# Attention scores: rotary high halves as paired 64-row products, and one maximum over four banks

## The chip, the cores and the metric

The kernel runs on one core of a Trainium2 chip. The metric is device time in microseconds (us) of one launch; the kernel before takes 2313.79 us, the median of 3 runs (2311.18 to 2315.13). The engines run their own instruction lists and meet through semaphores: TensorE (PE, matrix products; PEld is its weight load), VectorE (DVE), ScalarE (ACT), GpSimd (POOL) and SyncE (SP, which issues the transfers).

## The reference

Two layers of an encoder on 2048 tokens of width 1024, all in float32. The first is a retention branch beside an attention branch, the second a convolution module. The change lies in the attention: 4 heads, each query and key the concatenation of 128 plain and 64 rotary numbers, the rotary key shared by all heads, softmax over all 2048 keys.

```python
q = jnp.concatenate([q[..., :128], _rope(q[..., 128:], cos, sin)], axis=-1)
k = jnp.concatenate([k_nope, jnp.broadcast_to(k_rope, (B, S, MLA_HEADS, MLA_ROPE_DIM))], axis=-1)
s = jnp.einsum('bqhd,bkhd->bhqk', qblk, k, preferred_element_type=jnp.float32) * scale
p = jax.nn.softmax(s, axis=-1).astype(v.dtype)
o = jnp.einsum('bhqk,bkhd->bqhd', p, v)
```

## The kernel before

Products are made from float32 numbers that are each split into a rounded high part (type fp32r) and a low rest. A product of two split operands is the sum of low*high, high*low and high*high.

The function `attention` runs 16 groups n (4 heads of 4 groups of 512 queries), each in 4 blocks b of 128 queries. In a block, TensorE makes the scores of 128 queries against 2048 keys in four pieces of 512 keys (`scores`, kb 0 to 3), one PSUM bank each, of five products: plain low*high, high*low, two rotary ones, plain high*high. The rotary operand `q_rot` has the 64 high rows on partitions 0 to 63 and the 64 low rows on partitions 64 to 127. `kr_swap` holds the key's rotary parts as low over high and `kr_same` as high over low, so that a product of 128 rows with `kr_swap` gives high*low + low*high, and one with `kr_same` gives high*high + low*low.

Between the scores of block b, TensorE works on the group before: `turn` transposes the softmax weights (`probs`) of four key tiles kt, `values_of` multiplies them with the values. All orders are written out by hand. Per block: scores 0, turn 0, scores 1, turn 1, scores 2, scores 3, values -2, values -1, turn 2, values 0, turn 3, values 1; negative numbers are tiles that the block before has turned. Group 0 has no group before it, and in its odd blocks the scores go to the four other banks.

VectorE takes a maximum of each bank as it is finished (`block_max`), then one of the four results, and scales it to `bias` (`block_bias`); ScalarE takes the four exponentials (`exps`) in the block after, the first of them behind `turn_hi` of turn 2. `turn_hi` (ScalarE) and `turn_lo` (VectorE) split what TensorE has turned. Scores of piece kb wait until the exponential of the block before has read that bank (`exp_done`); turn kt waits for `turn_lo` of kt - 2 (`ptlo_done`).

In block 1 VectorE also splits the queries of the next group (`split_q`) and, in the group after a head's first, a quarter of the values (`split_v`), before `turn_lo` of tile 3. In block 3 it adds a piece of the second layer's modulation weights, loaded by SP in block 0, to the sum `acc`. The first queries are split earlier, in `q_high` and `q_low`.

Of the kernel before, what the change touches and what calls it, by code (L numbers as in the profile page):

```python
# [12 lines left out]
F32 = mybir.dt.float32  # L13
# [1381 lines left out]
def q_high(dve, begun, early, q_in):  # L1395
    q_st, qr_st = early[0:2]
    dve.wait_ge(q_in, 48)
    dve.tensor_copy(begun.q_rot[:], qr_st[:]).then_inc(begun.rot_hi, 1)
    dve.tensor_copy(begun.q_hi[:], q_st[:]).then_inc(begun.qhi_done, 1)


def q_low(dve, begun, early):
    q_st, qr_st = early[0:2]
    dve.wait_ge(begun.rot_hi, 1)
    dve.tensor_tensor(begun.q_rot[ROPE:P, :], qr_st[ROPE:P, :], begun.q_rot[ROPE:P, :].bitcast(F32),
                      ALU.subtract).then_inc(begun.rot_ready, 1)
    dve.wait_ge(begun.qhi_done, 1)
    dve.tensor_tensor(begun.q_lo[:], q_st[:], begun.q_hi[:].bitcast(F32), ALU.subtract).then_inc(begun.qlo_first, 1)


def first_scores(nc, ctx, base, early_at):

    KB = 1024
    f = Store()

    def at(name, offset, n):
        return nc.alloc_sbuf_tensor_at(name, [P, n], F32R, offset=offset)

# [12 lines left out]
    return f  # L1431


def attention(nc, st, ada_w, acc, kr_keep, early_at, early, k_in, q_in, begun, w_out, w_raw, w_lo, mix, mix_in, xt, x, x_in, out_stored):
# [4 lines left out]
    with ExitStack() as ctx:  # L1439
# [24 lines left out]
        q_hi, q_lo, q_rot = [[one] for one in (begun.q_hi, begun.q_lo, begun.q_rot)]  # L1464
        for name, pair in (("hi", q_hi), ("lo", q_lo), ("rot", q_rot)):
            sb(f"q_{name}_place", [P, GQ])
            pair.append(sb(f"q_{name}1", [P, GQ], F32R))
        probs = [[sb(f"probs{i}{b}", [P, S]) for b in range(QB)] for i in range(2)]
# [5 lines left out]
        ada = sb("ada2", [P, 3 * D // 2])  # L1474
        mx = sb("mx", [P, QB])
# [21 lines left out]
        max_done = sem("max_done")  # L1497
# [25 lines left out]
        ada_view = ada_w.rearrange("(k p) (a n) -> k a p n", p=P, a=2)  # L1523
# [39 lines left out]
        def bank_of(n, b, kb):  # L1563

            return (ps_pt + ps_o)[kb][:] if first(n) and b % 2 else ps_s[kb][:]
# [18 lines left out]
        def _(sp):  # L1584
# [12 lines left out]
            def group(n, s, score, values, write):  # L1597
# [4 lines left out]
                for b in range(QB):  # L1602
# [44 lines left out]
        def _(act):  # L1647
# [14 lines left out]
            def turn_hi(m, kt):  # L1662
                act.wait_ge(pt_done, 16 * m + kt + 1)
                if not (isinstance(m, int) and 16 * m + kt < 4):
                    act.wait_ge(pv_done, 16 * m + kt - 3)
                act.activation(pt_hi[kt % 4][:], ps_pt[kt % 2][:], ACT.Copy).then_inc(pthi_done, 1)  # L1666
# [11 lines left out]
            def group(n, s, score, values, write):  # L1678
                for b in range(QB):
# [13 lines left out]
                    if b == 1 and write:  # L1693
                        act.wait_ge(pv_done, 16 * (n - 1))
                        if not isinstance(n, int) or n > 2:
                            act.wait_ge(o_turned, n - 2)
                        act.activation(o_t[:], ps_o[s][:], ACT.Copy).then_inc(o_out, 1)
# [44 lines left out]
        def _(dve):  # L1742
# [6 lines left out]
            def split_q(m, sl):  # L1749
# [6 lines left out]
                dve.tensor_tensor(q_rot[sl][ROPE:P, :], qr_st[ROPE:P, :], q_rot[sl][ROPE:P, :].bitcast(F32),  # L1756
                                  ALU.subtract).then_inc(rot_ready, 1)
# [11 lines left out]
            def turn_lo(m, kt):  # L1769
                hold(dve, st, pthi_done, 16 * m + kt + 1)  # L1770
                dve.tensor_tensor(pt_lo[kt % 4][:], ps_pt[kt % 2][:], pt_hi[kt % 4][:].bitcast(F32),  # L1771
                                  ALU.subtract).then_inc(ptlo_done, 1)

            def group(n, s, score, values, write):
                for b in range(QB):
# [3 lines left out]
                    if b == 3 and score:  # L1779
                        hold(dve, st, ada_in, 16 * (n + 1))  # L1780
                        half = slice(s * 3 * D // 2, (s + 1) * 3 * D // 2)
                        if isinstance(n, int) and n < 2:
                            dve.tensor_scalar(acc[:, half], ada[:], st.silu_c[:, 0:1], None, ALU.mult).then_inc(acc_done, 1)
                        else:
                            hold(dve, st, acc_done, n - 1)
                            dve.scalar_tensor_tensor(acc[:, half], ada[:], st.silu_c[:, bass.ds(n // 2, 1)],
                                                     acc[:, half], ALU.mult, ALU.add).then_inc(acc_done, 1)
                    for i in range(4):
                        if score:
                            block_max(n, b, i)  # L1790
                        if i < 2 and turned:
                            turn_lo(turned[0], turned[1] + i)
# [30 lines left out]
        def _(pe):  # L1823
            def scores(n, s, b, kb):
# [24 lines left out]
                pe.matmul(dst, q_rot[s][:, q], kr_same[:, k], start=False, stop=False)  # L1849
                pe.matmul(dst, q_hi[s][:, q], k_hi[hs][:, k], start=False, stop=True).then_inc(s_done, 1)  # L1850
# [10 lines left out]
            def values_of(m, sl, kt):  # L1861
# [5 lines left out]
                pe.matmul(ps_o[sl][:], v_lo[:, kt, :], pt_hi[kt % 4][:], start=kt == 0, stop=False)  # L1867
                pe.matmul(ps_o[sl][:], v_hi[:, kt, :], pt_lo[kt % 4][:], start=False, stop=False)  # L1868
                pe.matmul(ps_o[sl][:], v_hi[:, kt, :], pt_hi[kt % 4][:], start=False, stop=kt == NK - 1).then_inc(pv_done, 1)  # L1869

            def group(n, s, score, values, write):
                for b in range(QB):
# [13 lines left out]
                    if score:  # L1886
# [5 lines left out]
                        scores(n, s, b, 3)  # L1892
                        values_next(-2)
# [1201 lines left out]
```

## Time and profile before

| | |
|---|---|
| median of 3 runs | 2313.79 us |
| the profiled execution's own time | 2312.47 us |
| its span (first to last instruction) | 2310.6 us |
| granted TensorE clock, mean share of full speed | 0.989 |
| TensorE busy, share of the span | 97% |
| VectorE, ScalarE, GpSimd busy | 59%, 49%, 39% |

The profile is of one execution. A busy matrix product is not TensorE at its peak: products are pipelined, so the distance between the starts of two of them, not the length of one, is what each costs. In a timeline row the bracket says how long the engine stood idle just before, and which instruction ended that.

### The profile page before, as it was taken

What the parts mean: (1) busy time and instruction counts of PE and PEld (TensorE: products, weight loads), DVE (VectorE), ACT (ScalarE), POOL (GpSimd) and SP (SyncE); (2) the same over time, 40 slices, a digit from 0 to 9 for tenths busy, and PEclk for the clock granted to TensorE, in tenths of its full rate; (3) what the DMA queues carried; (4) which work ended last, traced back from release to release, by engine and by line L of the source; (5) the groups of instructions that cost most, each with busy time, mean ns of one, the idle gap of its engine ahead of it and who ended that gap; (6) DMA issues with size and microseconds to landing.
All of it is one profiled execution on the core that took longest, in us unless ns stands there. A gap on an engine that the chain in (4) does not pass through costs nothing. (4 is left out here: it accounts for less than half of the span.)

```text
span 2310.6 us, 31013 instructions
## 1 busy us (share of the span) xinstructions
PE 2242.0 (97%) x11298; PEld 1884.8 (82%) x11298; DVE 1370.0 (59%) x2083; ACT 1125.9 (49%) x2095; POOL 900.6 (39%) x665
## 2 busy tenths in 40 slices
PE   5999999999999999999999989998999999999998
PEld 5888888898897788888888878887888888888886
DVE  7333336343435776767677642115999999994442
ACT  5555534222224555555555535556555566663432
POOL 6322222232222111101101023232999999992454
PEclk9999999999999999999999999999999999999999
DMA  7533323534444222222131323331111211145553
GB/s 304 183 136 136 136 78 132 173 120 151 137 149 141 56 65 69 65 69 65 32 83 33 105 105 112 134 118 37 46 55 42 69 55 42 64 167 163 157 172 101
DMA packets 151298, 245.75 MB, mean 106 GB/s; under 512 B 8964, under 2 KB 95236, under 8 KB 146566
## 3 DMA queue, kind: packets, MB, share of 16 engines
q1 hardware_dynamic: 146566, 235.73, 31.0%
q10 hardware_dynamic: 4608, 8.39, 1.0%
q8 instruction: 75, 1.23, 0.2%
q14 instruction: 49, 0.40, 0.1%
HBM read 157.84 MB, written 86.25 MB: 106 GB/s over the span
## 5 line engine op out<-in xcount | busy, mean ns | idle before, releaser
L2410 POOL TENSOR_TENSOR conv_g<-conv_g,product 128x1024 f32<-128x1024 f32 x160 | 385.0, 2408 | 34.2 <-ACT product L2459 24.5
L2554 DVE SCALAR_TENSOR_TENSOR ps_b<-u,cols,ps_b 128x1024 f32<-128x1024 f32 x304 | 391.7, 1288 | 9.2
L2670 PE MATMUL ps_a<-ho_hi,wp_lo 128*128 128x512 f32 x768 | 300.2, 391 | 6.8 <-DVE h_left L2610 6.8
L2671 PE MATMUL ps_a<-h_left,wp_hi 128*128 128x512 f32 x768 | 299.6, 390 | 0.0
L2672 PE MATMUL ps_a<-ho_hi,wp_hi 128*128 128x512 f32 x768 | 299.5, 390 | 0.0
L2459 ACT ACTIVATE product<-u,cols 128x1024 f32<-128x1024 f32 x160 | 183.3, 1151 | 170.3 <-POOL conv_g L2410 169.0
L1771 DVE TENSOR_TENSOR pt_lo<-ps_pt,pt_hi 128x512 fp32r<-128x512 f32 x256 | 176.1, 688 | 136.0 <-ACT pt_hi L1666 134.0
L1666 ACT ACTIVATE pt_hi<-ps_pt 128x512 fp32r<-128x512 f32 x256 | 154.4, 604 | 202.9 <-PE ps_pt L1858 202.1
L1761 DVE TENSOR_REDUCE mx<-ps_s 128x1 f32<-128x512 f32 x248 | 168.2, 683 | 34.3 <-PE ps_s L1850 32.6
L1659 ACT ACTIVATE probs<-ps_s,bias 128x512 f32<-128x512 f32 x248 | 168.8, 700 | 17.6 <-DVE bias L1767 9.3
L2670 PEld LDWEIGHTS ps_a<-ho_hi,wp_lo 128*128 128x128 f32 x768 | 144.6, 188 | 38.6 <-DVE h_left L2610 8.7
L2672 PEld LDWEIGHTS ps_a<-ho_hi,wp_hi 128*128 128x128 f32 x768 | 144.6, 188 | 30.1
L2671 PEld LDWEIGHTS ps_a<-h_left,wp_hi 128*128 128x128 f32 x768 | 144.4, 188 | 29.8
L1721 POOL TENSOR_TENSOR q_lo<-q_st,q_hi 128x512 fp32r<-128x512 f32 x15 | 26.9, 1793 | 342.6 <-DVE q_hi L1754 342.6
L1858 PEld LDWEIGHTS ps_pt<-const,probs 128*128 128x128 f32 x1024 | 127.0, 140 | 38.1 <-DVE pt_lo L1771 4.7
L1858 PE MATMUL ps_pt<-const,probs 128*128 128x128 f32 x1024 | 154.0, 273 | 2.1 <-DVE pt_lo L1771 2.1
L1846 PE MATMUL ps_s<-k_hi,q_lo 128*128 128x512 f32 x248 | 111.0, 448 | 7.6 <-ACT probs L1659 5.0
L1867 PE MATMUL ps_ot<-pt_hi,v_lo 128*128 128x512 f32 x256 | 111.9, 437 | 0.3 <-DVE pt_lo L1771 0.3
L2924 PE MATMUL ps_a<-w_last_hi,mo_lo 128*128 128x512 f32 x256 | 101.1, 395 | 1.8 <-PEq L2200 1.7
L1869 PE MATMUL ps_ot<-pt_hi,v_hi 128*128 128x512 f32 x256 | 100.7, 393 | 0.0
L1868 PE MATMUL ps_ot<-pt_lo,v_hi 128*128 128x512 f32 x256 | 100.2, 391 | 0.0
L2926 PE MATMUL ps_a<-w_last_hi,mo_hi 128*128 128x512 f32 x256 | 99.9, 390 | 0.0
(445 smaller groups left out, 5435.4 us busy)
## 6 DMA issues: line engine op xcount, KB each, us to landing
scratch_ret_pack<-pack SPq DMA_DIRECT2D x14, 1280.0 KB, 5.5
pack<-scratch_ret_pack SPq DMA_DIRECT2D x14, 1280.0 KB, 6.4
ada<-in_ada_w_dram SPq DMA_DIRECT2D x16, 768.0 KB, 6.1
wp_raw<-in_od_w_in_dram SPq DMA_DIRECT2D x24, 512.0 KB, 3.9
xt<-in_x_dram SPq DMA_DIRECT2D x16, 512.0 KB, 6.2
ada<-in_ada_w_dram SPq DMA_DIRECT2D x8, 1024.0 KB, 9.3
mix_e<-scratch_mix SPq DMA_DIRECT2D x16, 512.0 KB, 4.5
x_e<-in_x_dram SPq DMA_DIRECT2D x16, 512.0 KB, 5.0
```

The source lines that it names most:

```text
L1659: act.activation(probs[s][b][:, kb * BANK:(kb + 1) * BANK], bank_of(n, b, kb), ACT.Exp, bias=bias[b % 2][:], scale=SCALE, accum_out=sums[s ...
L1666: act.activation(pt_hi[kt % 4][:], ps_pt[kt % 2][:], ACT.Copy).then_inc(pthi_done, 1)
L1761: dve.tensor_reduce(mx[:, kb:kb + 1], bank_of(n, b, kb), AX.X, ALU.max).then_inc(max_done, 1)
L1771: dve.tensor_tensor(pt_lo[kt % 4][:], ps_pt[kt % 2][:], pt_hi[kt % 4][:].bitcast(F32), ALU.subtract).then_inc(ptlo_done, 1)
L1858: mm = pe.transpose(ps_pt[kt % 2][:, qb * P:(qb + 1) * P], probs[sl][qb][:, kt * P:(kt + 1) * P], ident)
L1867: pe.matmul(ps_o[sl][:], v_lo[:, kt, :], pt_hi[kt % 4][:], start=kt == 0, stop=False)
L2410: pool.tensor_tensor(half(conv_g, h), half(conv_g, h), product[adds(c, i, h) % 2][:], ALU.add).then_inc(added, 1)
L2459: act.activation(product[adds(c, i, h) % 2][:], units(c, V_TAPS + i, h), ACT.Copy, scale=tap_w).then_inc(product_done, 1)
L2554: dve.scalar_tensor_tensor(acc[h], units(c, k, h), params(c, k), acc[h], ALU.mult, ALU.add).then_inc(tap, 1)
L2670: pe.matmul(dst, lo[:, k, :], h_hi[:, k, t], start=k == 0, stop=False)
L2671: pe.matmul(dst, hi[:, k, :], h_lo[:, k, t], start=False, stop=False)
L2672: mm = pe.matmul(dst, hi[:, k, :], h_hi[:, k, t], start=False, stop=k == KD - 1)
```

## The change

The product with `kr_same` goes out of the five. In its place come, behind the four products of all four banks, four products of 64 rows (`high_scores`): banks 0 and 2 with the high rows of `q_rot` and `kr_same` on partitions 0 to 63, banks 1 and 3 with a new copy `q_high` of the high query rows and the high key rows of `kr_swap` on partitions 64 to 127. low*low is no longer computed. Only these four signal that a bank is ready. VectorE takes one maximum over the four banks in one instruction of 2048 columns, behind `turn_lo` 0 and 1. The cast of the rotary queries becomes two casts of 64 rows. The modulation weights come in pieces of 768 columns, in blocks 0 and 2, and are added in blocks 1 and 3.

```diff
+    f.q_high = at("q_high0", f.kr_at + 26 * KB, BANK)
-        ps_s = [bank(f"ps_s{i}") for i in range(4)]
-        ps_pt = [bank(f"ps_pt{i}") for i in range(2)]
-        ps_o = [bank(f"ps_ot{i}") for i in range(2)]
+        ps_all = [ctx.enter_context(nc.psum_tensor(n, [P, QB * BANK], F32)) for n in ("ps_scores", "ps_turned")]
+        banks = [[four[:, i * BANK:(i + 1) * BANK] for i in range(QB)] for four in ps_all]
+        ps_s, ps_pt, ps_o = banks[0], banks[1][0:2], banks[1][2:4]
...
-                    if b == 0 and score:
-                        hold(sp, st, acc_done, n)
-                        sp.dma_start(ada[:], ada_view[n // 2][s]).then_inc(ada_in, 16)
+                    if b % 2 == 0 and score:
+                        sp.wait_ge(acc_done, 2 * n + b // 2)
+                        sp.dma_start(ada[:], ada_view[n // 2][2 * s + b // 2]).then_inc(ada_in, 16)
...
-                dve.tensor_copy(q_rot[sl][:], qr_st[:]).then_inc(rot_hi, 1)
+                dve.tensor_copy(q_rot[sl][0:ROPE, :], qr_st[0:ROPE, :])
+                dve.tensor_copy(q_high[sl][ROPE:P, :], qr_st[ROPE:P, :]).then_inc(rot_hi, 1)
...
-            def block_max(n, b, kb):
-                hold(dve, st, s_done, 16 * n + 4 * b + kb + 1)
-                dve.tensor_reduce(mx[:, kb:kb + 1], bank_of(n, b, kb), AX.X, ALU.max).then_inc(max_done, 1)
-
             def block_bias(n, b):
-                hold(dve, st, max_done, 16 * n + 4 * b + 4)
-                dve.tensor_reduce(m1[:], mx[:], AX.X, ALU.max).then_inc(m1_done, 1)
+                dve.wait_ge(s_done, 16 * n + 4 * b + 4)
+                dve.wait_ge(bias_ready, 4 * n + b)
+                four = ps_all[1 if first(n) and b % 2 else 0]
+                dve.tensor_reduce(m1[:], four[:], AX.X, ALU.max).then_inc(m1_done, 1)
...
-                pe.matmul(dst, q_rot[s][:, q], kr_same[:, k], start=False, stop=False)
-                pe.matmul(dst, q_hi[s][:, q], k_hi[hs][:, k], start=False, stop=True).then_inc(s_done, 1)
+                pe.matmul(dst, q_hi[s][:, q], k_hi[hs][:, k], start=False, stop=False)
+
+            def high_scores(n, s, b):
+                q = slice(b * P, (b + 1) * P)
+                for kb in range(QB):
+                    k = slice(kb * BANK, (kb + 1) * BANK)
+                    if kb % 2 == 0:
+                        mm = pe.matmul(bank_of(n, b, kb), q_rot[s][0:ROPE, q], kr_same[0:ROPE, k], start=False, stop=True)
+                    else:
+                        mm = pe.matmul(bank_of(n, b, kb), q_high[s][ROPE:P, q], kr_swap[ROPE:P, k], start=False, stop=True)
+                    mm.then_inc(s_done, 1)
...
                         scores(n, s, b, 3)
+                        high_scores(n, s, b)
                         values_next(-2)
```

TensorE, scores 3 of a block and what follows them, before (`ps_s` is a score bank, `ps_ot` the output):

```order
L1846 MATMUL ps_s<-k_hi_1684,q_lo 128x512
L1847 MATMUL ps_s<-k_lo_1685,q_hi 128x512
L1848 MATMUL ps_s<-kr_swap,q_rot 128x512
L1849 MATMUL ps_s<-kr_same,q_rot 128x512
L1850 MATMUL ps_s<-k_hi_1684,q_hi 128x512
L1867 MATMUL ps_ot<-pt_hi,v_lo 128x512
```

The same place now (`ps_scores` are the four score banks, `ps_turned` the four others):

```order
L1850 MATMUL ps_scores<-k_hi_1684,q_lo 128x512
L1851 MATMUL ps_scores<-k_lo_1685,q_hi 128x512
L1852 MATMUL ps_scores<-kr_swap,q_rot 128x512
L1853 MATMUL ps_scores<-k_hi_1684,q_hi 128x512
L1860 MATMUL ps_scores<-kr_same,q_rot 128x512
L1862 MATMUL ps_scores<-kr_swap,q_high 128x512
L1860 MATMUL ps_scores<-kr_same,q_rot 128x512
L1862 MATMUL ps_scores<-kr_swap,q_high 128x512
L1880 MATMUL ps_turned<-pt_hi,v_lo 128x512
```

Each piece has one product fewer, and two pairs of half products stand between the last piece and the values.

VectorE, block 1 of a group after a head's first, from the second pair of maxima to the block after, before (`mx` holds the four maxima, `m` their maximum):

```order
L1761 TENSOR_REDUCE mx<-ps_s 128x1 x2
L1765 TENSOR_REDUCE m<-mx 128x1
L1767 TENSOR_SCALAR bias<-m 128x1
L1771 TENSOR_TENSOR pt_lo<-ps_pt,pt_hi 128x512
L1747 CAST v_hi<-v_st 128x512
L1753 CAST q_rot_1690<-qr_st 128x512
L1754 CAST q_hi_1688<-q_st 128x512
L1756 TENSOR_TENSOR q_rot_1690<-qr_st,q_rot_1690 64x512
L1771 TENSOR_TENSOR pt_lo<-ps_pt,pt_hi 128x512
L1761 TENSOR_REDUCE mx<-ps_s 128x1
```

The same place now:

```order
L1769 TENSOR_REDUCE m<-ps_scores 128x1
L1771 TENSOR_SCALAR bias<-m 128x1
L1775 TENSOR_TENSOR pt_lo<-ps_turned,pt_hi 128x512
L1752 CAST v_hi<-v_st 128x512
L1758 CAST q_rot_1690<-qr_st 64x512
L1759 CAST q_high_1691<-qr_st 64x512
L1760 CAST q_hi_1688<-q_st 128x512
L1762 TENSOR_TENSOR q_rot_1690<-qr_st,q_high_1691 64x512
L1775 TENSOR_TENSOR pt_lo<-ps_turned,pt_hi 128x512 x3
```

One cast more stands ahead of the first of the three `turn_lo` (that of tile 3), and the maximum is one instruction behind all of a block's scores.

## Rows read from the trace of the kernel before

**Rows 1.** Windows, one stretch of attention: length, busy of PE, PEld, DVE, ACT, POOL, clock, DMA.

```profile
1000.00:1050.00 50.00, 49.78 (x265) 41.00 (x263) 36.38 (x69) 27.87 (x67) 6.46 (x5) 1.00 0.32 89
```

**Rows 2.** Timeline, end of a block: start, length (us), engine, line, operation, count [idle].

```profile
1003.28 0.39 PE L1846 MATMUL ps_s<-k_hi,q_lo 128*128 128x512 f32 x1
...
1004.20 0.39 PE L1850 MATMUL ps_s<-k_hi,q_hi 128*128 128x512 f32 x1
...
1004.43 0.39 PE L1867 MATMUL ps_ot<-pt_hi,v_lo 128*128 128x512 f32 x1
...
1004.63 0.69 DVE L1761 TENSOR_REDUCE mx<-ps_s 128x1 f32<-128x512 f32 x1 [0.40 <-PE ps_s L1850]
...
1005.36 0.16 DVE L1765 TENSOR_REDUCE m<-mx 128x1 f32<-128x4 f32 x1
1005.55 0.15 DVE L1767 TENSOR_SCALAR bias<-m 128x1 f32<-128x1 f32 x1
...
1006.93 0.68 ACT L1659 ACTIVATE probs<-ps_s,bias 128x512 f32<-128x512 f32 x1
...
1007.50 0.20 ACT L1659 ACTIVATION_READ_ACCUMULATOR probs<-ps_s,bias 128x1 f32 x1
...
1008.07 0.40 PE L1846 MATMUL ps_s<-k_hi,q_lo 128*128 128x512 f32 x1
```

**Rows 3.** Timeline, the retention's products of 64 rows, and their neighbours on PE.

```profile
705.68 0.27 PE L1275 MATMUL ps_tr<-const,rot 128*64 128x128 f32 x1
705.88 0.37 PE L1315 MATMUL ps_s<-pack 64*128 64x128 f32 x1
...
706.09 0.27 PE L1315 MATMUL ps_s<-pack 64*128 64x128 f32 x1
...
706.20 0.27 PE L1315 MATMUL ps_s<-pack 64*128 64x128 f32 x1
...
706.32 0.27 PE L1315 MATMUL ps_s<-pack 64*128 64x128 f32 x1
706.32 0.27 PE L1315 MATMUL ps_o<-pack 64*128 64x128 f32 x1
706.52 0.50 PE L1247 MATMUL ps_mg<-wi_hi,h_lo 128*128 128x512 f32 x1
706.86 0.40 PE L1248 MATMUL ps_mg<-wi_lo,h_hi 128*128 128x512 f32 x1
```

**Rows 4.** One line (L1315): PE's idle time before it, us and times.

```profile
  issue: 3.0, 15
```

**Rows 5.** Timeline, the first two block ends of group 1.

```profile
762.01 0.69 DVE L1761 TENSOR_REDUCE mx<-ps_s 128x1 f32<-128x512 f32 x1 [0.44 <-PE ps_s L1850]
...
763.12 0.69 ACT L1659 ACTIVATE probs<-ps_s,bias 128x512 f32<-128x512 f32 x1 [1.75 <-DVE bias L1767]
...
763.95 0.50 PE L1846 MATMUL ps_s<-k_hi,q_lo 128*128 128x512 f32 x1 [1.97 <-ACT probs L1659]
...
771.35 0.69 DVE L1761 TENSOR_REDUCE mx<-ps_s 128x1 f32<-128x512 f32 x1 [0.39 <-PE ps_s L1850]
...
772.46 0.69 ACT L1659 ACTIVATE probs<-ps_s,bias 128x512 f32<-128x512 f32 x1
...
773.42 0.39 PE L1846 MATMUL ps_s<-k_hi,q_lo 128*128 128x512 f32 x1
```

**Rows 6.** Timeline, blocks 1 and 2 of a group after a head's first.

```profile
1073.42 0.42 DVE L1753 CAST q_rot<-qr_st 128x512 fp32r<-128x512 f32 x1
...
1073.59 1.41 POOL L1717 TENSOR_TENSOR v_lo<-v_st,v_hi 128x512 fp32r<-128x512 f32 x1 [8.40 <-DVE v_hi L1747]
1073.76 1.52 DVE L1754 CAST q_hi<-q_st 128x512 fp32r<-128x512 f32 x1
...
1076.39 0.39 PE L1850 MATMUL ps_s<-k_hi,q_hi 128*128 128x512 f32 x1
...
1076.77 0.66 PE L1858 MATMUL ps_pt<-const,probs 128*128 128x128 f32 x4
```

More of the change, by code:

```diff
@@ L1397, in q_high @@
     dve.wait_ge(q_in, 48)
-    dve.tensor_copy(begun.q_rot[:], qr_st[:]).then_inc(begun.rot_hi, 1)
+    dve.tensor_copy(begun.q_rot[0:ROPE, :], qr_st[0:ROPE, :])
+    dve.tensor_copy(begun.q_high[ROPE:P, :], qr_st[ROPE:P, :]).then_inc(begun.rot_hi, 1)
     dve.tensor_copy(begun.q_hi[:], q_st[:]).then_inc(begun.qhi_done, 1)
@@ L1404, in q_low @@
     dve.wait_ge(begun.rot_hi, 1)
-    dve.tensor_tensor(begun.q_rot[ROPE:P, :], qr_st[ROPE:P, :], begun.q_rot[ROPE:P, :].bitcast(F32),
+    dve.tensor_tensor(begun.q_rot[ROPE:P, :], qr_st[ROPE:P, :], begun.q_high[ROPE:P, :].bitcast(F32),
                       ALU.subtract).then_inc(begun.rot_ready, 1)
@@ L1464, in attention @@
         q_hi, q_lo, q_rot = [[one] for one in (begun.q_hi, begun.q_lo, begun.q_rot)]
+        q_high = [begun.q_high]
         for name, pair in (("hi", q_hi), ("lo", q_lo), ("rot", q_rot)):
             sb(f"q_{name}_place", [P, GQ])
+            if name == "rot":
+                sb("q_high_place", [P, GQ])
             pair.append(sb(f"q_{name}1", [P, GQ], F32R))
+        q_high.append(sb("q_high1", [P, GQ], F32R))
         probs = [[sb(f"probs{i}{b}", [P, S]) for b in range(QB)] for i in range(2)]
@@ L1473, in attention @@
         gate = sb("gate_in", [P, QB, DV])
-        ada = sb("ada2", [P, 3 * D // 2])
-        mx = sb("mx", [P, QB])
+        AQ = 3 * D // 4
+        ada = sb("ada2", [P, AQ])
         m1 = sb("m1", [P, 1])
@@ L1522, in attention @@
         mix_view = st.mix.rearrange("(g b p) (h d) -> h g p b d", p=P, b=QB, d=DV)
-        ada_view = ada_w.rearrange("(k p) (a n) -> k a p n", p=P, a=2)
+        ada_view = ada_w.rearrange("(k p) (a n) -> k a p n", p=P, a=4)
         block = ctx.enter_context(nc.Block())
@@ L1563, in bank_of @@
         def bank_of(n, b, kb):
-            return (ps_pt + ps_o)[kb][:] if first(n) and b % 2 else ps_s[kb][:]
+            return banks[1 if first(n) and b % 2 else 0][kb]
         def last(n, k):
@@ L1665, in turn_hi @@
                     act.wait_ge(pv_done, 16 * m + kt - 3)
-                act.activation(pt_hi[kt % 4][:], ps_pt[kt % 2][:], ACT.Copy).then_inc(pthi_done, 1)
+                act.activation(pt_hi[kt % 4][:], ps_pt[kt % 2], ACT.Copy).then_inc(pthi_done, 1)
             def w_piece(n, b, i):
@@ L1696, in group @@
                             act.wait_ge(o_turned, n - 2)
-                        act.activation(o_t[:], ps_o[s][:], ACT.Copy).then_inc(o_out, 1)
+                        act.activation(o_t[:], ps_o[s], ACT.Copy).then_inc(o_out, 1)
                     if score and next_keys(n, b):
@@ L1778, in group @@
                         turn_lo(*left_over(n, b, values, write))
[L1779 to L1783, printed above, removed]
-                        else:
-                            hold(dve, st, acc_done, n - 1)
-                            dve.scalar_tensor_tensor(acc[:, half], ada[:], st.silu_c[:, bass.ds(n // 2, 1)],
-                                                     acc[:, half], ALU.mult, ALU.add).then_inc(acc_done, 1)
+                    if b % 2 and score:
+                        at = 2 * s + b // 2
+                        dve.wait_ge(ada_in, 16 * (2 * n + b // 2 + 1))
+                        part = slice(at * AQ, (at + 1) * AQ)
+                        if n < 2:
+                            dve.tensor_scalar(acc[:, part], ada[:], st.silu_c[:, 0:1], None, ALU.mult).then_inc(acc_done, 1)
+                        else:
+                            dve.wait_ge(acc_done, 2 * n + b // 2 - 3)
+                            dve.scalar_tensor_tensor(acc[:, part], ada[:], st.silu_c[:, n // 2:n // 2 + 1],
+                                                     acc[:, part], ALU.mult, ALU.add).then_inc(acc_done, 1)
+                    for i in range(2):
+                        if turned:
+                            turn_lo(turned[0], turned[1] + i)
                     for i in range(4):
[L1789 to L1792, printed above, removed]
                         if i == 3 and score:
@@ L1866, in values_of @@
                     pe.wait_ge(out_ready, m - 1)
-                pe.matmul(ps_o[sl][:], v_lo[:, kt, :], pt_hi[kt % 4][:], start=kt == 0, stop=False)
-                pe.matmul(ps_o[sl][:], v_hi[:, kt, :], pt_lo[kt % 4][:], start=False, stop=False)
-                pe.matmul(ps_o[sl][:], v_hi[:, kt, :], pt_hi[kt % 4][:], start=False, stop=kt == NK - 1).then_inc(pv_done, 1)
+                pe.matmul(ps_o[sl], v_lo[:, kt, :], pt_hi[kt % 4][:], start=kt == 0, stop=False)
+                pe.matmul(ps_o[sl], v_hi[:, kt, :], pt_lo[kt % 4][:], start=False, stop=False)
+                pe.matmul(ps_o[sl], v_hi[:, kt, :], pt_hi[kt % 4][:], start=False, stop=kt == NK - 1).then_inc(pv_done, 1)
             def group(n, s, score, values, write):
```

5 lines of the change are left out of this document (2 added, 3 removed).

## The prediction

> **What bounds the kernel now.** The page's first part has TensorE busy through the whole span, so I went to the stage of the change and asked for windows of 50 us in it. The one of 1000 to 1050 [rows 1] is typical: TensorE is busy 49.8 of 50 us at the full clock, VectorE 36.4, ScalarE 27.9. TensorE's own list sets the pace, and time is gained only where it gets shorter. Then the timeline of one block end, for two things. The price of a product of 512 columns: five of them start between 1003.28 and 1004.43, so 0.23 us each [rows 2]. And the cover: the last maximum starts 0.43 us behind the start of the last score product, that is, when the product has landed, and TensorE begins the next block's scores 3.44 us after that, with values and turns in between. Within those 3.44 us maximum, bias and the first exponential must be through [rows 2]. Third, the timeline around the retention's products of 64 rows, the only ones in this trace that use half the array [rows 3, 4], for the price of changing to such products and back.
>
> **The change, part by part.**
>
> *Products removed.* In each of 64 blocks four products of 128 rows go and four of 64 rows come. In the retention the two halves of a pair start together (706.32 and 706.32) and the pairs follow each other by 0.11 us, what one such product alone would take [rows 3]. So a pair costs one product, and two pairs two: 2 x 0.23 = 0.46 us less per block, 64 x 0.46 = 29.4 us.
>
> *Going into the half array and out again.* The first pair starts 0.20 us behind the product before it in place of 0.11, and the second 0.21 behind the first (705.68, 705.88, 706.09): 0.09 + 0.10 = 0.19 us lost. On the way out the next full product starts 0.20 us behind the last pair in place of 0.11, and its successor 0.34 behind it in place of 0.23: 0.20 us lost [rows 3]. No wait on another engine ends that idle time: 3.0 us in 15 tiles, 0.20 each, put down to issue [rows 4]. The first halves look like the array running empty, the second like a weight load that was not made ahead. I take the same sums behind products of 512 columns, since both concern what comes after the last column has gone in: 64 x 0.19 + 63 x 0.20 = 24.8 us (one way out lies in a wait, below). Bounds: 0.21 us per block, 13.4 us, if only the weight loads could be made ahead here; nothing, if neither loss occurs; twice the sum, if the wait grows with the length of the products. I take the middle because all 16 tiles have the same numbers.
>
> The Trainium skill, TensorE: Matmul & The Clock Gate, Part 3 (packing small matmuls), has TensorE pulling a weight load ahead of products in flight when it aims at rows not in use or at the background buffer. By that the two exposed loads would go, and 64 x 0.21 = 13.4 us with them. The trace does not agree where the row mode changes: 0.21 and 0.34 in place of 0.11 and 0.23 [rows 3]; there the load waits.
>
> So this part of the list, which is the point of the change, gains 29.4 - 24.8 = 4.6 us, 0.07 us per block.
>
> *One maximum of 2048 columns.* 512 columns take 0.69 us, 4 columns 0.16 [rows 2]: 1.04 ns a column, so 2048 take 0.16 + 2044 x 0.00104 = 2.29 us. Bounds: 2.13 (the columns alone) and 4 x 0.69 = 2.76. Before, the exponential could start 1.11 us after the last maximum began (762.01 to 763.12) [rows 5]; the maximum of the four, 0.16 + 0.03, goes, so now it is 2.29 + 1.11 - 0.69 - 0.19 = 2.52 us. From the exponential's start to the next scores it is 0.57 to its second instruction, 0.20 for that, 0.05 to TensorE: 0.82 [rows 2]. Sum 3.34. The cover was 3.44 and grows by the 0.20 of the way out, to 3.64: 0.30 us to spare, nothing lost. In block 0 and 1 the first exponential has further cover. VectorE itself spends less than before (2.29 for 4 x 0.69 + 0.16), and it is not the bound.
>
> *Where the cover is thinner.* Group 1 has no values to multiply yet. Its block 0 has no cover at all: TensorE waits 1.97 us there already [rows 5], and the later bias comes on top: 2.52 - 1.11 = 1.4 us. In its block 1 TensorE is back at scores 2.07 us after the maximum begins (771.35 to 773.42) [rows 5], now 2.27; 3.34 are needed: 1.07 of waiting and 0.11 for the weight load behind it, 1.2 us.
>
> *One cast more, in block 1.* Where a quarter of the values is split in the same block (groups 1, 5, 9, 13), the cast of `q_hi` takes 1.52 us in place of 0.42, as long as GpSimd's split of the values runs (1073.59 for 1.41), and TensorE's turn 1 of block 2 starts at 1076.77, where 1076.39 + 0.23 = 1076.62 was due [rows 6]: it already waits 0.15 for `turn_lo` of tile 3, queued behind the casts. Now the list on VectorE comes 0.20 later (turn 2 lies behind the way out), the second cast is the one that waits for GpSimd, and `q_hi` adds its 0.34 (1073.42 to 1073.76) behind it: 0.54 later. TensorE is there 2 x 0.23 - 0.20 = 0.26 earlier. The wait grows by 0.80 us, four times: 3.2 us. In the other groups, without the 1.1 us of standing behind GpSimd, the wait stays away.
>
> *The modulation weights* come in halves of the size, one a block earlier than the other; each is asked for two blocks, some 18 us, ahead of its use, and the additions stand ahead of the maximum, where VectorE waits for TensorE anyway. I cost them, and the first split of the queries (one cast more, while TensorE makes the last keys and queries), at nothing; if the cover were gone it would be 0.34 us once for the cast and the 0.1 us by which two additions are longer than one, per group.
>
> *Sum.* -29.4 + 24.8 + 1.4 + 1.2 + 3.2 = +1.2 us on the profiled execution's 2312.47 us (a span of 2310.6 and 1.9 around it, which stays): 2313.7. The median of the runs is 1.3 us above that execution, so the forecast is 2315 us.
>
> **The rivals.**
>
> *The way in and out is cheaper.* For it: two pairs of 512 columns give the sequencer more time to load ahead than products of 128; the loads in [rows 3] stand between operations of another type. Against: the same 0.20, 0.21 and 0.34 in all tiles. Without the exposed loads the time is 2315 - 13.4 = 2302; without any loss 2315 - 24.8 = 2290.
>
> *The bias comes too late* (slower). If the one maximum costs what four do, 2.76 us, exponentials are ready 3.81 us after it begins, and the cover is 3.64. Every second block (2 and 3; block 1 has the turning of the output as cover, block 0 a later exponential) then waits 0.17 + 0.11 for the weight load, 30 x 0.28 = 8.4 us, and group 1 another 0.9: 2324. It decides from a maximum of 2.59 us on. For it: 0.30 us is little, and anything in front of the maximum on VectorE eats it. Against: VectorE is idle when the scores land, 0.40 us before the maximum of [rows 2].
>
> *The pairs do not overlap at 512 columns*, since two streams of results into two banks at full rate are in no row here; the retention's pairs are shorter and of another type. Then 29.4 us come back: 2344. [...]
>
> **How the numbers follow.** The forecast holds with 0.45, its own range 2310 to 2320; the cheaper way in and out 0.28; the late bias 0.17; pairs in a row 0.06; 0.04 for what I don't see. What a measurement can tell from no change is 0.2%, 4.6 us, so faster is below 2309.2 and slower above 2318.4. Faster: 0.26 of the first rival and 0.06 of the forecast, 0.32. Slower: 0.17 + 0.06 + 0.03 + 0.08 of the forecast, 0.34. Same: 0.34. The range of 8 in 10 takes in the hidden weight loads and the late bias: 2301 to 2325.
>
> **What the profile of the changed kernel would show.** The two halves of a pair start within 0.01 us and the pairs 0.33 apart (0.23 + 0.10); the first values 0.32 behind the second pair; the maximum 2.3 us long. Idle time of TensorE before scores: 3.4 us in group 1's block 0, 1.1 in its block 1, hardly any in the steady blocks; before turn 1 of block 2 about 0.9 in four groups. A steady group of four blocks takes 0.3 us less than before. The forecast is wrong if the pairs start 0.46 apart, if the first full product behind them is not late, or if scores wait for exponentials in every group's blocks 3 and 0.

## The result

| | before | after |
|---|---|---|
| median of 20 runs each on one chip | 2310.27 us | 2316.19 us |
| ratio, with its 95% interval | | 1.0023 (1.0016 to 1.0030) |
| the profiled execution's own time, its span | 2312.47, 2310.6 us | 2313.11, 2311.2 us |

The changed kernel is slower by 0.23%, 5.3 us (3.7 to 6.9). The forecast was +1.2 us on the profiled execution, 2315 us; the result lies in its range, and 4 us above its sum. That 2315 comes within 1.2 us of 2316.19 is luck: the three runs it was counted from have a median 3.5 us above that of the twenty, and this hides most of what the sum is short. The two profiled executions differ by only 0.6 us: that pair must not be subtracted as a whole, as the second profile of the kernel before shows below.

The window that answers to [rows 1] shows the same picture, TensorE without a gap:

```profile
1000.00:1050.00 50.00, 49.77 (x267) 38.63 (x266) 35.90 (x55) 29.18 (x73) 7.46 (x5) 1.00 0.28 80
```

The timeline of one block end of the changed kernel, which answers to [rows 2] (start, length in us, engine, line):

```profile
1005.99 0.39 PE L1853 MATMUL ps_scores<-k_hi,q_hi 128*128 128x512 f32 x1
...
1006.31 0.49 PE L1860 MATMUL ps_scores<-kr_same,q_rot 64*128 64x512 f32 x1
1006.31 0.49 PE L1862 MATMUL ps_scores<-kr_swap,q_high 64*128 64x512 f32 x1
...
1006.64 0.39 PE L1860 MATMUL ps_scores<-kr_same,q_rot 64*128 64x512 f32 x1
...
1006.97 0.19 PEld L1880 LDWEIGHTS ps_turned<-pt_hi,v_lo 128*128 128x128 f32 x1 [0.36 <-issue]
1006.97 0.50 PE L1880 MATMUL ps_turned<-pt_hi,v_lo 128*128 128x512 f32 x1
...
1007.11 2.29 DVE L1769 TENSOR_REDUCE m<-ps_scores 128x1 f32<-128x2048 f32 x1 [1.22 <-PE ps_scores L1862]
1007.31 0.39 PE L1881 MATMUL ps_turned<-pt_lo,v_hi 128*128 128x512 f32 x1
...
1009.62 0.69 ACT L1664 ACTIVATE probs<-ps_scores,bias 128x512 f32<-128x512 f32 x1
...
1010.72 0.40 PE L1850 MATMUL ps_scores<-k_hi,q_lo 128*128 128x512 f32 x1
```

Read the distances between starts on TensorE: 0.23 between full products, 0.32 into the first pair, 0.33 to the second, 0.32 out, 0.34 to the product behind, 0.23 again. The halves of a pair start together. The four excesses over 0.23 are 0.09, 0.10, 0.09 and 0.11. The first weight load behind the pairs starts with its product, after 0.36 us in which it waited for no other engine. The maximum takes 2.29 us and the first exponential starts 2.51 us after it began; the next scores do not wait.

Group 1 and a group that follows a head's first, TensorE's waits of the changed kernel in the timeline (answering to [rows 5, 6]):

```profile
764.81 0.78 PE L1850 MATMUL ps_scores<-k_hi,q_lo 128*128 128x512 f32 x1 [3.42 <-ACT probs L1664]
...
775.32 0.50 PE L1850 MATMUL ps_scores<-k_hi,q_lo 128*128 128x512 f32 x1 [1.00 <-ACT probs L1664]
...
779.11 0.66 PE L1871 MATMUL ps_turned<-const,probs 128*128 128x128 f32 x4 [1.23 <-DVE pt_lo L1775]
...
925.65 1.40 POOL L1722 TENSOR_TENSOR v_lo<-v_st,v_hi 128x512 fp32r<-128x512 f32 x1 [8.37 <-DVE v_hi L1752]
925.91 1.43 DVE L1759 CAST q_high<-qr_st 64x512 fp32r<-64x512 f32 x1
...
927.38 0.43 DVE L1760 CAST q_hi<-q_st 128x512 fp32r<-128x512 f32 x1
...
929.30 0.66 PE L1871 MATMUL ps_turned<-const,probs 128*128 128x128 f32 x4 [0.91 <-DVE pt_lo L1775]
```

In block 0 the wait grows from 1.97 to 3.42, in block 1 from nothing to 1.00. The cast that stands behind GpSimd's product is now `q_high`, and the wait for `pt_lo` is 0.91.

How long a group takes is read from one product that comes once in each group, the first scores of block 1. Before, then after:

```profile
876.67 0.50 PE L1846 MATMUL ps_s<-k_hi,q_lo 128*128 128x512 f32 x1 [0.22 <-ACT probs L1659]
914.14 0.50 PE L1846 MATMUL ps_s<-k_hi,q_lo 128*128 128x512 f32 x1 [0.22 <-ACT probs L1659]
951.76 0.50 PE L1846 MATMUL ps_s<-k_hi,q_lo 128*128 128x512 f32 x1 [0.22 <-ACT probs L1659]
```

```profile
879.03 0.50 PE L1850 MATMUL ps_scores<-k_hi,q_lo 128*128 128x512 f32 x1 [0.23 <-ACT probs L1664]
916.29 0.50 PE L1850 MATMUL ps_scores<-k_hi,q_lo 128*128 128x512 f32 x1 [0.23 <-ACT probs L1664]
954.73 0.50 PE L1850 MATMUL ps_scores<-k_hi,q_lo 128*128 128x512 f32 x1 [0.23 <-ACT probs L1664]
```

A steady group takes 37.26 in place of 37.47 us (-0.21), a group that follows a head's first 38.44 in place of 37.62 (+0.82; the two others +0.78 and +0.76). Ten of the one and three of the other cancel: from the first turning of an output to the last it is 534.41 us before and 534.64 after. (The 0.22 or 0.23 us in the brackets is a wait that both kernels have once a group, at the end of block 0.) What is left is group 1, from its first scores to those of group 2 34.98 us before (757.28 to 792.26) and 38.24 after (756.80 to 795.04): +3.3, in its blocks 0, 1 and 2 by 1.3, 1.0 and 0.9. And the first split of the queries, below.

### The profile page after: what moved, and what is told of

It reads as the page before. It is cut to its first block and busy times, and to the rows that moved or that the text cites. A ratio compares the mean times of both kernels' runs of the same rounds, so it can differ in the third digit from the quotient of the medians.

```text
span 2311.2 us, 30883 instructions
## 1 busy us (share of the span) xinstructions
PE 2235.0 (97%) x11298; PEld 1847.8 (80%) x11298; DVE 1360.7 (59%) x1859; ACT 1124.5 (49%) x2095; POOL 898.5 (39%) x665
## 3 DMA queue, kind: packets, MB, share of 16 engines
q8 instruction: 75, 1.23, 0.2%
## 5 line engine op out<-in xcount | busy, mean ns | idle before, releaser
L1671 ACT ACTIVATE pt_hi<-ps_turned 128x512 fp32r<-128x512 f32 x256 | 153.9, 602 | 198.8 <-PE ps_turned L1871 197.0
L1775 DVE TENSOR_TENSOR pt_lo<-ps_turned,pt_hi 128x512 fp32r<-128x512 f32 x256 | 176.3, 691 | 108.5 <-ACT pt_hi L1671 101.1
L1769 DVE TENSOR_REDUCE m<-ps_scores 128x1 f32<-128x2048 f32 x62 | 142.1, 2292 | 75.6 <-PE ps_scores L1862 75.5
L1664 ACT ACTIVATE probs<-ps_scores,bias 128x512 f32<-128x512 f32 x248 | 168.5, 696 | 18.7 <-DVE bias L1771 10.5
L1871 PEld LDWEIGHTS ps_turned<-const,probs 128*128 128x128 f32 x1024 | 126.9, 140 | 42.5 <-DVE pt_lo L1775 8.4
L1871 PE MATMUL ps_turned<-const,probs 128*128 128x128 f32 x1024 | 154.1, 273 | 5.8 <-DVE pt_lo L1775 5.8
L1850 PE MATMUL ps_scores<-k_hi,q_lo 128*128 128x512 f32 x248 | 110.8, 447 | 10.1 <-ACT probs L1664 7.6
L1880 PE MATMUL ps_turned<-pt_hi,v_lo 128*128 128x512 f32 x256 | 118.7, 464 | 0.3 <-DVE pt_lo L1775 0.3
L1882 PE MATMUL ps_turned<-pt_hi,v_hi 128*128 128x512 f32 x256 | 100.9, 394 | 0.0
L1881 PE MATMUL ps_turned<-pt_lo,v_hi 128*128 128x512 f32 x256 | 100.1, 391 | 0.0
```

The costliest lines, as they stand in the source:

```text
L1664: act.activation(probs[s][b][:, kb * BANK:(kb + 1) * BANK], bank_of(n, b, kb), ACT.Exp, bias=bias[b % 2][:], scale=SCALE, accum_out=sums[s ...
L1671: act.activation(pt_hi[kt % 4][:], ps_pt[kt % 2], ACT.Copy).then_inc(pthi_done, 1)
L1775: dve.tensor_tensor(pt_lo[kt % 4][:], ps_pt[kt % 2], pt_hi[kt % 4][:].bitcast(F32), ALU.subtract).then_inc(ptlo_done, 1)
L1871: mm = pe.transpose(ps_pt[kt % 2][:, qb * P:(qb + 1) * P], probs[sl][qb][:, kt * P:(kt + 1) * P], ident)
```

## The experiments

Times are medians. `again`, `casts_moved`, `full_rows` and `two_bursts` ran on one chip with the kernel before at 2309.79; `one_max_alone`, `extra_max`, `best` and `before_again` on a second with it at 2310.88; `one_half` on a third with it at 2309.97.

**The changed kernel once more, `again`** (no edit).

> The changed kernel once more, for a second profile on the chip that the next three run on. If its loss against the kernel before is made of fixed pieces (group 1, four groups with casts, the first split of the queries), all stages show the same times as in its first profile: 37.26 to 37.29 us a steady group, 38.4 a group that follows a head's first, and the time is some 5 us over the kernel before. If the difference of the two medians (5.9 us) comes from stages in which the granted clock happened to differ, a stage that the change doesn't touch differs again, and the time may be as near to the kernel before as the two first profiles were (0.6 us).

Measured: 2317.09 us, 1.0026 (1.0016 to 1.0035) of the kernel before. Steady groups 37.26, the others 38.39, group 1's waits 3.42 and 1.00: fixed. But the granted clock from 370 to 390 us, in the retention, is 0.86 in place of 0.94, and attention begins at 739.76 in place of 738.76. So both readings hold: the loss has fixed pieces, and beside them one execution differs from the next by a us or two where nothing was touched.

**The kernel before once more, `before_again`** (no edit).

> The kernel before once more, for a second profile of it: how far the stages that the change doesn't touch differ between two executions of the same code. The first scores began at 737.6 us in its first profile and at 738.1 to 741.7 in five profiles with the change, and the stage behind attention lost 1 to 2 us in its first profile alone. If that belongs to the executions and not to the code, the second profile has other numbers there by 1 to 3 us, and the same 37.47 and 37.62 us in the groups. Its time is that of the kernel before within 0.1%.

Measured: 2310.95 us, 0.9998 (0.9989 to 1.0007). One window of its second profile, and the same of the first (length, busy of PE, PEld, DVE, ACT, POOL, clock, DMA):

```profile
740.00:770.00 30.00, 28.03 (x132) 22.94 (x131) 22.40 (x47) 16.50 (x45) 7.65 (x5) 1.00 0.54 156
```

```profile
740.00:770.00 30.00, 28.03 (x120) 22.75 (x118) 20.90 (x43) 15.66 (x43) 7.64 (x5) 0.93 0.53 154
```

The same code, and the granted clock differs: 0.93 in the first profile and 1.00 in the second here, 0.95 and 0.87 from 370 to 390 us, 0.61 and 1.00 in the 4 us behind a wait at 723 to 724 us (below). From its first scores to the first turning of an output the first profile took 73.34 us and the second 70.37: 1.40 of the difference lies in the first block of group 0 (6.05 and 4.65), 1.59 in the block behind group 1's first wait (9.47 and 7.88). The first profile of before was unlucky there, and this hid group 1's loss in the pair of profiles: 73.34 before against 74.92 after. The groups are the same, 37.47 and 37.62. The stage behind attention is the same too, 965.2 and 965.0 us from the last turning of an output to the end, so what I expected there did not come: the changed kernel's profiles have 962.9 and 963.9, the other versions with the same code there 962.8 to 965.1.

**Full products in the burst, `full_rows`.**

```diff
-                    if kb % 2 == 0:
-                        mm = pe.matmul(bank_of(n, b, kb), q_rot[s][0:ROPE, q], kr_same[0:ROPE, k], ...)
-                    else: ...
+                    mm = pe.matmul(bank_of(n, b, kb), q_rot[s][:, q], kr_same[:, k], start=False, stop=True)
```

> The changed kernel with the burst made of four full products of 128 rows (one per bank) in place of two pairs of 64 rows: no change to half the array and back, all else as it is. If pairs cost 0.23 us each and the way in and out 0.39 a block, a block gets 0.46 - 0.39 = 0.07 us longer: a steady group 37.26 + 0.28 = 37.5 us, the whole 4.5 us slower than the changed kernel. If the way in and out costs as much as the pairs save (0.46), there is no difference. If the way in were half hidden, 64 x 0.2 = 13 us slower.

Measured: 2318.53 us, 1.4 over `again` and 2.3 over the changed kernel; a steady group 37.46 to 37.50, 0.22 longer than with pairs. Two pairs in place of four products (0.46 us less in a block) are worth 0.055. The theory stands, with even less left for the pairs than the forecast's 0.07; the way in and out eats 0.40 of the 0.46. (The 0.055 is a mean: 0.14 in block 0, where a late bias adds to it as under `one_max_alone`, and 0.02 to 0.04 in the others. Against the kernel before, the changed one gains 0.05 to 0.06 in every block.)

**Two bursts of one pair, `two_bursts`.**

```diff
                         scores(n, s, b, 1)
+                        high_scores(n, s, b, (0, 1))
                         turn_next(1)
...
-                        high_scores(n, s, b)
+                        high_scores(n, s, b, (2, 3))
```

> The changed kernel with the burst cut in two: the pair of banks 0 and 1 behind the scores of bank 1, the pair of banks 2 and 3 behind those of bank 3. The same four products, but twice into half the array and twice out of it. By the sums from the retention (0.09 in, 0.20 out for each change, and 0.10 for the second pair, which a burst of one pair doesn't have) a block has 2 x (0.09 + 0.20) = 0.58 in place of 0.39 of loss: 64 x 0.19 = 12 us slower than the changed kernel. If a lone pair pays the whole 0.39, it is 25 us slower. If the change of rows is free and the exposed 0.1 belongs to every pair, nothing changes.

Measured: 2337.82 us, 21 over `again`; a steady group 38.73 (+1.47, 0.37 a block). The timeline of the second burst, which now holds one pair:

```profile
1008.30 0.39 PE L1853 MATMUL ps_scores<-k_hi,q_hi 128*128 128x512 f32 x1
...
1008.62 0.49 PE L1860 MATMUL ps_scores<-kr_same,q_rot 64*128 64x512 f32 x1
...
1009.05 0.50 PE L1880 MATMUL ps_turned<-pt_hi,v_lo 128*128 128x512 f32 x1
...
1009.39 0.40 PE L1881 MATMUL ps_turned<-pt_lo,v_hi 128*128 128x512 f32 x1
```

In is 0.32 (0.09 over 0.23) as with two pairs; out is 0.43 (0.20 over), where it was 0.32 behind a second pair; then 0.34 (0.11 over). That is 0.40 again: the 0.10 of the second pair is no price of a pair, it belongs to the change of rows and falls on whatever comes second. The second reading fits, the others are out.

**One half of the array, `one_half`.**

```diff
-                    if kb % 2 == 0:
-                        mm = ... q_rot[s][0:ROPE, q], kr_same[0:ROPE, k] ...
-                    else:
-                        mm = ... q_high[s][ROPE:P, q], kr_swap[ROPE:P, k] ...
+                    mm = pe.matmul(bank_of(n, b, kb), q_rot[s][0:ROPE, q], kr_same[0:ROPE, k], start=False, stop=True)
```

> The changed kernel with all four 64-row products of the burst on the same half of the array (rows 0 to 63 for every bank; the same sums come out, since both halves held the same operands), so nothing overlaps: is the way in and out a price of going to 64 rows, or of two streams at once? If it is the change of rows alone (0.09 in, 0.20 out) and loads of the same half are made ahead, the burst takes 4 x 0.23 + 0.29 = 1.21 in place of 0.86 us: 0.36 a block, 23 us slower than the changed kernel. If each product of 64 rows pays the exposed 0.10 as each pair did, it takes 4 x 0.33 + 0.30 - 0.10 = 1.52: 0.66 a block, 42 us slower. If only overlapping pairs pay, 4 x 0.23 = 0.92: 0.06 a block, 4 us slower.

Measured: 2347.39 us, 31 over the changed kernel, 0.49 a block; no one of the three. The timeline:

```profile
1013.91 0.39 PE L1853 MATMUL ps_scores<-k_hi,q_hi 128*128 128x512 f32 x1
1014.23 1.19 PE L1859 MATMUL ps_scores<-kr_same,q_rot 64*128 64x512 f32 x4
1015.35 0.50 PE L1877 MATMUL ps_turned<-pt_hi,v_lo 128*128 128x512 f32 x1
1015.69 0.39 PE L1878 MATMUL ps_turned<-pt_lo,v_hi 128*128 128x512 f32 x1
```

0.32 in; 1.12 from the first of the four to the values, which is 4 x 0.23 + 0.20; then 0.34. So the loss is again 0.09 + 0.20 + 0.11 = 0.40, once and not per product, and without any overlap: it is the price of changing rows. Four products in a row take 4 x 0.23 + 0.40, two pairs 2 x 0.23 + 0.40: the pairs overlap whole. (The first reading came nearest; its sum had left out the 0.10 of the second product.)

**One maximum alone, `one_max_alone`** (the five full products and the one cast as before; what stays are the maximum over four banks and the halves of the modulation weights).

```diff
+                pe.matmul(dst, q_rot[s][:, q], kr_same[:, k], start=False, stop=False)
+                pe.matmul(dst, q_hi[s][:, q], k_hi[hs][:, k], start=False, stop=True).then_inc(s_done, 1)
...
-                        high_scores(n, s, b)
```

> The changed kernel without the pairs: the five full products per bank as before, one cast of the rotary queries as before; what is left of the change is the one maximum of 2048 columns and the modulation weights in halves. If the maximum is hidden in the steady blocks as forecast (cover 3.44 us without the way out, chain 3.34) and costs only in group 1 (1.4 in block 0, and 1.07 + 0.20 = 1.3 in block 1), it is 2.7 us slower than the kernel before, steady groups 37.47, and as fast as the changed kernel or up to 2 us faster. If the late bias is behind the loss, scores wait for exponentials in blocks 2 and 3 of every group, a steady group takes more than 37.6, and it is over 5 us slower than the kernel before.

Measured: 2315.52 us, 1.0022 (1.0013 to 1.0031), 5.1 (3.0 to 7.2) over the kernel before. The first wait in group 1, timeline:

```profile
765.05 0.79 PE L1848 MATMUL ps_scores<-k_hi,q_lo 128*128 128x512 f32 x1 [3.38 <-ACT probs L1663]
```

3.38, and 1.11 behind it, as forecast. But a steady group takes 37.57 to 37.60, 0.12 longer than before, where I had expected none: 0.09 to 0.10 of it in block 0 (9.60 us in place of 9.50), the rest in block 3. 14 x 0.12 = 1.7 us. The timeline where one block 3 ends and the next block 0 begins:

```profile
828.77 2.29 DVE L1767 TENSOR_REDUCE m<-ps_scores 128x1 f32<-128x2048 f32 x1 [1.00 <-PE ps_scores L1852]
...
831.29 0.69 ACT L1663 ACTIVATE probs<-ps_scores,bias 128x512 f32<-128x512 f32 x1
...
832.18 0.19 PEld L1848 LDWEIGHTS ps_scores<-k_hi,q_lo 128*128 128x128 f32 x1 [0.25 <-issue]
832.21 0.47 PE L1848 MATMUL ps_scores<-k_hi,q_lo 128*128 128x512 f32 x1
...
832.52 0.39 PE L1849 MATMUL ps_scores<-k_lo,q_hi 128*128 128x512 f32 x1
```

The exponential starts 2.52 us behind the maximum, as in the chain of the forecast, and ends at 832.06. The load for the next scores did not start with the product ahead (831.98), but at 832.18; the scores are late by 0.02 and the product behind them by 0.08 (0.31 in place of 0.23). With the cover at 3.44, a chain worked out as 3.34 is too long by this. The changed kernel has 0.20 more from the way out of the half array; `full_rows`, without it, has 9.58 in block 0 too. The result lies between the two readings: group 1 as in the first, a late bias in the steady groups as in the second, though at the end of block 3 alone and not at its price. One maximum alone loses as much as the whole change; in its profile some 0.5 us lies in the first split of the queries, which is that of the kernel before (below).

**One more maximum in front, `extra_max`.**

```diff
+                dve.tensor_reduce(mx[:, 0:1], four[:, 0:BANK], AX.X, ALU.max)
                 dve.tensor_reduce(m1[:], four[:], AX.X, ALU.max).then_inc(m1_done, 1)
```

> The changed kernel with one more maximum over the first 512 columns (0.69 us, its result not used) in front of each block's maximum. By the chain of 3.34 us and the cover of 3.64 the bias has 0.30 us to spare, so 0.39 of the 0.69 show, with 0.11 for the weight load behind the wait: 0.50 us in blocks 2 and 3 of 14 groups, 14 us, and 2 x 0.69 in group 1: 15 us slower than the changed kernel. If the bias already is at its limit (nothing to spare), all 0.69 + 0.11 show: 22 + 1.4 = 24 us. If there is more cover than I counted, 2 us or less.

Measured: 2333.81 us, 17.6 over the changed kernel (15 forecast). TensorE's waits in attention (us in total, times, longest; 7.6 and 16 in the changed kernel):

```profile
PE ps_scores L1852 <- ACT probs L1665: 14.7, 45, 4.0
```

A steady group takes 38.25 to 38.33; blocks 2 and 3 are 0.42 and 0.51 us longer, 0.50 forecast. Less 0.11 for the weight load, 0.31 and 0.40 of the 0.69 show, so 0.29 to 0.38 were to spare: the bias would be late soon, but it is not in the steady blocks of the changed kernel.

**The casts one block later, `casts_moved`.**

```diff
+                    if score and not last(n, 1) and b == 2:
+                        split_q(n + 1, 1 - s)
...
-                    if score and not last(n, 1) and b == 1:
-                        split_q(n + 1, 1 - s)
```

(on VectorE right behind `turn_lo` of the tile left over; on GpSimd in block 2 too)

> The changed kernel with the split of the next group's queries (VectorE's casts and GpSimd's subtraction) one block later, in block 2 behind turn_lo of the tile left over. If the casts behind GpSimd's product are what costs four groups about 1 us each, TensorE's waits of 0.91 us for pt_lo (three of them) and 1.23 in group 1 go, the four groups come down from 38.4 to about 37.4 us, and the kernel is 4 us faster than the changed one, about 1 us slower than the kernel before. If these groups are late for another reason (splitting the values), the waits stay and the time too. A third way: the casts stand in front of turn_lo of block 2 and the waits come back there in all groups, 0.3 to 0.9 us in 15 groups, 5 to 13 us slower than the changed kernel.

Measured: 2315.67 us, 1.4 below `again` and not 4 (one of its eleven runs took 3545.65 us, which nothing here explains). In the profile the waits for `pt_lo` of 0.91 and 1.23 are gone, three of the four groups are at 37.26 like all others, group 1 takes 36.57 in place of 38.28, and attention takes 607.57 us against 611.07 in `again`. That is 3.5 less, one new wait at the first scores of group 1 included:

```profile
762.86 0.50 PE L1850 MATMUL ps_scores<-k_hi,q_lo 128*128 128x512 f32 x1 [1.44 <-POOL q_lo L1726]
```

So the casts are what cost these groups. The 3.5 of the profile and the 1.4 of the medians do not contradict each other, since the two versions are over the kernel before by 3.7 to 8.1 and 3.0 to 7.4 us.

**The losses taken out, `best`**: the casts as above but for group 0, blocks 0 and 1 of group 1 as in the kernel before, and in the first split

```diff
-    dve.tensor_copy(begun.q_high[ROPE:P, :], qr_st[ROPE:P, :]).then_inc(begun.rot_hi, 1)
     dve.tensor_copy(begun.q_hi[:], q_st[:]).then_inc(begun.qhi_done, 1)
...
 def q_low(dve, begun, early):
+    dve.tensor_copy(begun.q_high[ROPE:P, :], qr_st[ROPE:P, :]).then_inc(begun.rot_hi, 1)
```

> The changed kernel with its losses taken out: the split of the next queries in block 2 behind turn_lo (group 0 keeps it in block 1, since there GpSimd had it behind the split of the values and the scores of group 1 waited 1.4 us for it), the first split's new cast put behind the cast of q_hi, and blocks 0 and 1 of group 1 as in the kernel before (five full products a bank, four maxima). If the loss is group 1, the casts and the first split, what is left is the steady gain: 14 groups by 0.21 = 2.9 us, and about 0.3 from the groups that follow a head's first: 3 to 4 us faster than the kernel before, 2306 to 2307. If something else makes the changed kernel slower (a lower clock, for instance), it is 1 us or more slower than the kernel before.

Measured: 2308.27 us, 0.9988 (0.9979 to 0.9997) of the kernel before, 2.8 us faster (0.7 to 4.9). Attention, timeline: group 1's wait, and the product that comes once a group.

```profile
761.91 0.50 PE L1867 MATMUL ps_scores<-k_hi,q_lo 128*128 128x512 f32 x1 [2.07 <-ACT probs L1666]
...
873.63 0.50 PE L1867 MATMUL ps_scores<-k_hi,q_lo 128*128 128x512 f32 x1 [0.23 <-ACT probs L1666]
910.92 0.50 PE L1867 MATMUL ps_scores<-k_hi,q_lo 128*128 128x512 f32 x1 [0.23 <-ACT probs L1666]
```

2.07 in place of 3.42, and every group at 37.28 to 37.30. With these three places mended the time agrees with the pairs' gain being what is left (2.9 us and some 0.3); the interval leaves room for a us or two of something else. This version beats both kernels, the one before by little.

## Why the prediction was right in its steps and short in its sum

| term | forecast | measured |
|---|---|---|
| pairs, with the way in and out, a block | -0.46 + 0.39 = -0.07 | -0.05 |
| one maximum, steady blocks | 0 | 0 behind the pairs, 0.12 a group without them |
| group 1: block 0, block 1, casts | +1.4, +1.2, +0.8 | +1.3, +1.0, +0.9 (net of the pairs) |
| one cast more, three further groups | +0.80 each | +0.97 to 1.03 each (0.76 to 0.82, and 0.21) |
| first split of the queries | 0 | +0.85 with the clock down behind it, +1.7 at full clock |

*The way in and out* at the middle of its bounds was right: the retention's 0.09, 0.10, 0.09 and 0.11 [rows 3] came back behind products four times as long. By the Trainium skill, TensorE: Matmul & The Clock Gate, Part 3, loads that aim at rows not in use or at the background buffer would be pulled ahead; here too the trace does not agree, with 0.33 and 0.34 in place of 0.23. [rows 4] I read wrongly: its 3.0 us are the weight load's idle time on the way in, not TensorE's on the way out. For the way out the changed kernel's load shows the same, 0.36 put down to issue. The cheaper way falls, with 0.40 in each kind of burst; pairs in a row fall too. The size of what is left was off by a third, 0.05 for 0.07, because it is the small difference of two numbers that were rounded to 0.01: over 64 blocks 1.1 us less gain.

*One maximum, nothing lost* held: 2.29 us long as forecast, no wait in steady blocks that the kernel before has not, and `extra_max` shows the 0.30 to spare. *The bias too late*, the slower rival, is not the cause.

*One cast more* was the right mechanism, too small by 0.2 each: block 2 was 0.15 us over that of a steady group and is 1.13 over it now. Half of the 0.2 lies in the list on VectorE, which from `v_hi` to `pt_lo` takes 3.39 us in place of 2.94, 0.45 more where I had counted 0.34. Of the casts only the first runs undisturbed beside GpSimd; the second is held to the end of GpSimd's product, and the third comes behind it.

*The first split of the queries at nothing* is the step that failed. I named TensorE's keys and queries as its cover, and did not look for who waits for the same VectorE list. The timeline of the changed kernel:

```profile
719.57 1.67 POOL L1117 TENSOR_TENSOR pack<-pack 128x512 f32<-128x512 f32 x1 [0.16 <-DVE pack L1184]
719.68 0.41 DVE L1398 CAST q_rot<-qr_st 64x512 fp32r<-64x512 f32 x1
...
720.10 1.42 DVE L1399 CAST q_high<-qr_st 64x512 fp32r<-64x512 f32 x1
...
722.23 0.41 DVE L1198 TENSOR_TENSOR rs<-ps_s,sin 128x256 f32<-128x256 f32 x1
...
723.78 0.62 PE L1274 MATMUL ps_tr<-const,rot 128*128 128x128 f32 x2 [2.71 <-POOL rot L1121]
```

and the same place before:

```profile
719.23 2.01 POOL L1117 TENSOR_TENSOR pack<-pack 128x512 f32<-128x512 f32 x1 [0.22 <-DVE pack L1184]
719.34 0.42 DVE L1398 CAST q_rot<-qr_st 128x512 fp32r<-128x512 f32 x1
...
719.67 0.41 DVE L1399 CAST q_hi<-q_st 128x512 fp32r<-128x512 f32 x1
...
722.69 0.44 PE L1274 MATMUL ps_tr<-const,rot 128*128 128x128 f32 x2 [1.91 <-POOL rot L1121]
```

`rs`, which GpSimd's `rot` needs and TensorE behind it, now stands behind a cast of 1.42 us, and TensorE waits 0.80 longer. In all seven profiles with this cast the product behind the wait comes 0.74 to 0.81 later against those ahead of it than in the first profile of before. And the list is late for a second reader, TensorE's queries, which wait for `heads_t`; `again`:

```profile
728.07 0.50 PE L1291 MATMUL ps_tq<-ct_hi,uq_lo 128*128 128x512 f32 x1 [0.93 <-DVE heads_t L1214]
```

Neither profile of before has this wait. What both cost is seen only where the clock is the same. In the 4 us behind the first wait it is 1.00 in the second profile of before and in `again`; the window of `again`:

```profile
725.21:729.21 4.00, 3.07 (x14) 2.28 (x15) 3.88 (x6) 2.62 (x7) 2.36 (x2) 1.00 0.20 66
```

At full clock it is 16.35 us from the start of the last L1291 product (the queries') ahead of the wait to attention's first scores in the second profile of before, and 18.10 in `again` (18.05 in `casts_moved` and `two_bursts`, at 1.00 too): +1.7. In the first profile of before the clock is 0.61 there and it is 17.69, in that of the changed kernel 0.57 and 18.54: +0.85. With the cast moved (`best`) TensorE waits 1.68 for `rot`, but still 0.92 for `heads_t`, and it is 17.06, so 0.7 is left. The cast is not all of it: in `one_max_alone`, which has the first split of the kernel before, the small `rs<-kr,sin` ahead of the casts took 1.33 in place of 0.21, TensorE waited 2.42, and it was 18.25 at a clock of 0.57, 0.56 longer than in the first profile of before. So this place can lose half a us without the cast.

*The sum* by stages: group 0 -0.2, group 1 +3.3, from the first output to the last +0.2, the first split 0.85 to 1.7: +4.1 to +5.0. The comparison says 5.3 (3.7 to 6.9), so no further cause is needed. The 3.3 is taken from two profiles whose clock fell behind group 1's wait; the second profile of before, where it did not, takes 33.37 us for the group, and against it the loss is 4.9. How often the clock falls in the runs that were only timed, nothing here shows.

## What to carry to other kernels

Products of half the rows save time only beyond the price of leaving the full array, which here was one fixed sum per burst: gather them or don't begin, and trust a small difference of two large terms only as far as their rounding. For each instruction added to a list, look for what another engine runs at that moment, and for who is queued behind it. Look for the pass of the pipeline that has no cover yet, and compare two kernels stage by stage over several profiles: here stages without a change differed by more than the change was worth.

## What the runs showed of the hardware

The price of a burst of 64-row products did not depend on their number, nor on overlap: 0.40 us with one pair, with two, and with four on one half. Of VectorE's casts beside a product of GpSimd some take 0.41 to 0.43 us and some 1.42 to 1.52, to the end of that product: in the first split both ran at 0.41 to 0.42 before, and with one cast more the second was caught. GpSimd's own product there took 2.01 us beside two undisturbed casts, 1.67 beside one, and 1.31 in `one_max_alone`, where VectorE's instruction was caught ahead of the casts: what VectorE does not wait, GpSimd seems to. What decides which is caught, no run here shows. And a wait can cost again behind itself. After group 1's first wait TensorE ran at half its clock, 1.2 GHz, for up to some 3 us in ten of the eleven profiles: in all eight with a wait of 3.4 to 4.0 us, and in two of the three with one of 2.0 to 2.1. Windows of some 3 us from the wait's end, of the changed kernel (wait 3.42 us), the first profile of before (1.97) and its second (1.97):

```profile
765.00:768.00 3.00, 3.00 (x10) 2.41 (x11) 0.00 (x0) 2.00 (x7) 0.94 (x1) 0.50 0.48 131
```

```profile
764.00:767.00 3.00, 3.00 (x10) 2.50 (x11) 0.69 (x1) 2.02 (x7) 0.78 (x1) 0.59 0.00 0
```

```profile
762.80:766.00 3.20, 3.20 (x19) 2.66 (x19) 1.40 (x3) 2.46 (x7) 0.79 (x1) 1.00 0.00 0
```

The granted clock is 0.50, 0.59 and 1.00; behind the same wait the same code fell once and once not, and the block behind it took 9.47 us with the fall and 7.88 without.
